# Tile 0's tokens in strips of 32 partitions: packed state products and updates, conv on unfolded copies

## The reference, cut to what matters

```python
cross = jnp.einsum('bhqd,bhdv->bhqv', q * q_dec[None, :, :, None], s)
s_new = (jnp.exp(c * log_g)[None, :, None, None] * s
         + jnp.einsum('bhkd,bhkv->bhdv', k * k_dec[None, :, :, None], v))
...
u = u_a * jax.nn.sigmoid(u_b)
ext = jnp.concatenate([conv_buf.astype(u.dtype), u], axis=1)
c = lax.conv_general_dilated(ext, conv_w[:, None, :], ...)
```

## Time and profile before

| | |
|---|---|
| runs, median | 1305.79 us (1303.9 to 1307.8) |
| profiled execution | 1306.49 us |
| its span in the trace | 1304.7 us |
| mean granted TensorE clock | 0.962 |
| PE busy | 1186.6 us, 91% |
| VectorE busy | 996.3 us, 76% |
| ACT busy | 632.8 us, 48% |
| POOL busy | 121.9 us, 9% |

### The profile page before, as it was taken

The page is one execution under the profiler, slowest core; times in us unless marked ns, Lnnn a source line. Parts: engine busy times, 40 slices in busy tenths (PEclk is TensorE's granted clock), DMA queues, the critical chain, the costliest instruction groups (busy, mean ns, idle before and its releaser), DMA issues.

```text
span 1304.7 us, 15355 instructions
## 1 busy us (share of the span) xinstructions
PE 1186.6 (91%) x5825; PEld 909.9 (70%) x5825; DVE 996.3 (76%) x1301; ACT 632.8 (48%) x565; POOL 121.9 (9%) x216
## 2 busy tenths in 40 slices
PE   3999999999999999999736999999999999999960
PEld 3985986798589759998524767676767677676740
DVE  3598779778986986465644888888888888888846
ACT  2350324134122502453114777777777777777740
POOL 3111020112012011000030000000000000000012
PEclk9999999999999999999857999999999999999985
DMA  8565483466347545345345999999999999999934
GB/s 213 179 209 193 125 262 125 178 201 234 117 178 228 196 176 174 129 129 192 130 134 211 356 373 380 388 377 381 381 382 379 381 380 380 381 382 380 388 95 109
DMA packets 171052, 332.25 MB, mean 255 GB/s; under 512 B 8154, under 2 KB 45322, under 8 KB 170960
## 3 DMA queue, kind: packets, MB, share of 16 engines
q1 hardware_dynamic: 150576, 264.41, 57.9%
q0 software_dynamic: 20400, 66.81, 15.2%
HBM read 295.28 MB, written 36.63 MB: 254 GB/s over the span
## 4 chain that ended last, share of the span: by engine, by line
PE 84%; DVE 7%; DMA 3%; ACT 3%; issue 2%; POOL 2%; POOLq 0%; DVEq 0%; ACTq 0%
PE bank L676 77%; PE bank L888 4%; PE bank L717 3%; DMA v2rows<-in_b_conv_o_dram 1%; DVE o_tok L1360 1%; DMA x_slots<-x,slot 1%; DMA y_back<-y_slots,slot 1%; DVE sg_lo L1374 1%; DVE sg_f L1372 1%; POOL x_slots L633 1%; ACT sg_hi L1074 1%; DMA y_slots<-yo 0%; POOL vrows L520 0%; DVE stats L1351 0%; DVE lo L996 0%
## 5 line engine op out<-in xcount | busy, mean ns | idle before, releaser
L1516 DVE TENSOR_TENSOR mlo<-mraw,mhi 128x2048 fp32r<-128x2048 f32 x192 | 439.5, 2290 | 79.1 <-ACT mhi L1140 75.8
L1140 ACT ACTIVATE mhi<-mraw 128x2048 fp32r<-128x2048 f32 x192 | 367.5, 1915 | 93.8 <-PE bank L676 83.7
L676 PE MATMUL bank<-mhi,xg_hi 128*96 128x512 f32 x512 | 203.2, 397 | 1.4 <-DVE xg_lo L1521 1.4
L676 PE MATMUL bank<-mhi,xg_lo 128*96 128x512 f32 x512 | 203.0, 397 | 0.0
L676 PE MATMUL bank<-mlo,xg_hi 128*96 128x512 f32 x512 | 201.7, 394 | 0.0
L996 DVE TENSOR_TENSOR lo<-raw,hi 128x2048 fp32r<-128x2048 f32 x56 | 128.3, 2290 | 83.2 <-ACT hi L1103 38.7
L991 ACT ACTIVATE hi<-raw 128x2048 fp32r<-128x2048 f32 x47 | 90.0, 1914 | 191.4 <-PE bank L676 191.4
L676 PE MATMUL bank<-xT_hi,hi 128*128 128x336 f32 x512 | 165.3, 323 | 6.4 <-DVE lo L996 6.4
L676 PE MATMUL bank<-xT_hi,lo 128*128 128x336 f32 x512 | 163.1, 319 | 0.0
L676 PE MATMUL bank<-xT_lo,hi 128*128 128x336 f32 x512 | 163.0, 318 | 0.0
L1269 DVE SCALAR_TENSOR_TENSOR cT<-E,hv,cT 128x272 f32<-128x272 f32 x480 | 150.3, 388 | 0.0
(11 more groups left out here) (245 smaller groups left out, 1572.9 us busy)
## 6 DMA issues: line engine op xcount, KB each, us to landing
mraw<-in_w_gate_dram SPq DMA_DIRECT2D x64, 1024.0 KB, 11.2
mraw<-in_w_up_dram SPq DMA_DIRECT2D x64, 1024.0 KB, 11.1
mraw<-in_w_down_dram SPq DMA_DIRECT2D x64, 1024.0 KB, 11.9
raw<-in_w_in_dram SPq DMA_DIRECT2D x40, 1024.0 KB, 5.3
st<-in_state_ret_dram POOLq DMA_DIRECT2D x32, 512.0 KB, 4.8
out_dram<-st POOLq DMA_DIRECT2D x32, 512.0 KB, 3.9
raw<-in_w_ret_o_dram SPq DMA_DIRECT2D x8, 1024.0 KB, 7.1
x_slots<-zeros POOLq DMA_DIRECT2D x12, 512.0 KB, 4.7
```

The costliest lines, as they stand in the source:

```text
L676: i = pe.matmul(out, a, b, start=s, stop=e)
L1140: act.activation(mhi[:, v % MH, :], mraw[:, v % MR, :], ACT.Copy).then_inc(mhi_ready, 1)
L1516: dve.tensor_tensor(mlo[:, v % MH, :], mraw[:, v % MR, :], mhi[:, v % MH, :].bitcast(f32), ALU.subtract).then_inc(mlo_ready, 1)
```

## The change

The tokens of tile 0 are put in another order: strip c (partitions 32c to 32c + 31) holds samples c and c + 4 in its first 16 places and, for c under 3, 16 prompt tokens behind them. Tile 0 still has 112 tokens. Tables follow (`token_order`); loads and stores of x and y for tile 0 become one per sample, one for the meta tokens, one for each 16 prompt tokens.

The state product takes 16 columns of `qdiag` a sample, into partitions 32c of the bank, four strips after one another for each r (sample c + 4r) and p. The state update asks for room for the four groups of an (r, p) first, then issues for each of the three terms four matmuls, each contracted over one strip's 32 rows; `kds` has one column of the table for each r, so 2 in place of 8.

The conv reads `W`, in which each 8 tokens have a window of their own with the 30 values before them (42 windows of 38): a tap is one instruction of 336 elements. VectorE writes u into the windows' ends with one instruction a half; ACT makes from it `us`, the prompt's stream `E`, and from that the first 30 places of the prompt's windows.

```diff
-        kds_hi = sb("kds_hi", [TT, NB, 256], f32r)
+        kds_hi = sb("kds_hi", [TT, 2, 256], f32r)
-        qdiag = sb("qdiag", [128, 2, NB * (NS + NI)])
+        qdiag = sb("qdiag", [128, 2, NB, QC])
...
-                     + [f"Pst{b}{p}" for b in range(NB) for p in range(2)]
+                     + [f"Pst{c + 4 * r}{p}" for r in range(2) for p in range(2) for c in range(4)]
...
+        def windows(c):
+            return W[:, c, :].rearrange("p (n w) -> p n w", n=NW)
+
+        def prompt_windows(c, j0, j1):
+
+            a = E[:, c, NI * j0:NI * j1 + CW - 1 - NI]
+            return bass.AP(a.tensor, a.offset, [list(a.ap[0]), [NI, j1 - j0], [1, CW - 1]])
+
+        def seq_windows(c):
+
+            w = windows(c)
+            return w[:, 0:16, :].rearrange("p (c r) w -> p c r w", c=4)[:, :, 0:2, :]
...
-            sp.dma_start(x_in[0:NS, 0, :], x_sample.rearrange("b i d -> (b i) d")).then_inc(s_x, 16)
-            sp.dma_start(x_in[NS:NS + NM, 0, :], meta_tokens).then_inc(s_x, 16)
-            sp.dma_start(x_in[NS + NM:TT, 0, :], x_prompt[0, 0:TT - NS - NM, :]).then_inc(s_x, 16)
+            for b in range(NB):
+                sp.dma_start(x_in[place(b):place(b) + NI, 0, :], x_sample[b]).then_inc(s_x, 16)
+            sp.dma_start(x_in[16:32, 0, :], meta_tokens).then_inc(s_x, 16)
+            for c in range(1, 3):
+                sp.dma_start(x_in[32 * c + 16:32 * c + 32, 0, :], x_prompt[0, 16 * c - NM:16 * c + 16 - NM, :]).then_inc(s_x, 16)
...
-                for c in range(2):
-                    pe.wait_ge(evac[HEAD.bank[f"ua{c}"]], HEAD.used(f"ua{c}", h) + 1)
+                pe.wait_ge(stream_ready, h * 2 + 2)
...
-                        o64 = bank[HEAD.bank[name]][0:NS, :]
-                        for b in range(NB):
+                        for r in range(2):
                             for p in range(2):
-                                i = pe.matmul(o64, qdiag[:, p, b * NS:(b + 1) * NS], st[:, b, p, :], start=False, stop=(b == NB - 1 and p == 1), skip_group_check=True)
+                                for c in range(4):
+                                    i = pe.matmul(bank[HEAD.bank[name]][32 * c:32 * c + QC, :], qdiag[:, p, c + 4 * r, :], st[:, c + 4 * r, p, :],
+                                                  start=False, stop=(r == 1 and p == 1), skip_group_check=True)
                         i.then_inc(group_done, 1)
...
-                for b in range(NB):
+                for r in range(2):
                     for p in range(2):
-                        name = f"st{b}{p}"
-                        room(HEAD, name, h)
-                        out, cols = bank[HEAD.bank[name]][:, :], slice(p * 128, (p + 1) * 128)
-                        group(HEAD, name, h, [(out, kds_hi[:, b, cols], v_hi[:, :], True, False), (out, kds_hi[:, b, cols], v_lo[:, :], False, False),
-                                              (out, kds_lo[:, b, cols], v_hi[:, :], False, True)])
+                        cols = slice(p * 128, (p + 1) * 128)
+                        for c in range(4):
+                            room(HEAD, f"st{c + 4 * r}{p}", h)
+                        for n, (a, v) in enumerate(((kds_hi, v_hi), (kds_hi, v_lo), (kds_lo, v_hi))):
+                            for c in range(4):
+                                rows = slice(32 * c, min(32 * c + 32, TT))
+                                i = pe.matmul(bank[HEAD.bank[f"st{c + 4 * r}{p}"]][:, :], a[rows, r, cols], v[rows, :], start=n == 0, stop=n == 2)
+                                if n == 2:
+                                    i.then_inc(group_done, 1)
...
+                for c in range(2):
+                    act.wait_ge(*took(HEAD, f"ua{c}", h))
+                    act.activation(us[:, c, :].rearrange("p (r c i) -> p c r i", r=2, c=4), seq_windows(c)[:, :, :, CW - 1:WW], ACT.Copy)
+                    act.activation(E[:, c, CW - 1:CW - 1 + 48].rearrange("p (c r i) -> p c r i", c=3, r=2), early_windows(c)[:, :, :, CW - 1:WW], ACT.Copy)
+                    act.activation(E[:, c, CW - 1 + 48:EXT].rearrange("p (n i) -> p n i", i=NI), windows(c)[:, 14:NW, CW - 1:WW], ACT.Copy).then_inc(stream_ready, 1)
+                    act.wait_ge(stream_ready, h * 2 + (c + 1))
+                    act.activation(early_windows(c)[:, :, :, 0:CW - 1], prompt_windows(c, 0, 6).rearrange("p (c r) w -> p c r w", c=3), ACT.Copy)
+                    act.activation(windows(c)[:, 14:NW, 0:CW - 1], prompt_windows(c, 6, 34), ACT.Copy).then_inc(windows_ready, 1)
...
-                for s in range(NB):
+                for s in range(2):
                     i = act.activation(kds_hi[:, s, :], b[0:TT, 0:256], ACT.Copy, scale=hs[0:TT, HKS + s:HKS + s + 1])
...
-                parts = [(out[:, NS:T], lambda w: E[:, c, EL + w:EL + w + NP]),
-                         (out[:, 0:NS].rearrange("p (b i) -> p b i", b=NB), lambda w: samples(E[:, c, :])[:, :, w:w + NI])]
                 for w in range(w0, w1):
                     tap = hv[:, VCW + c * CW + w:VCW + c * CW + w + 1]
-                    for q, (o, src) in enumerate(parts):
-                        if w == 0:
-                            ins = dve.tensor_scalar(o, src(w), tap, hv[:, VCB + c:VCB + c + 1], ALU.mult, ALU.add)
-                        else:
-                            dve.wait_ge(dve_step, conv_last[q])
-                            ins = dve.scalar_tensor_tensor(o, src(w), tap, o, ALU.mult, ALU.add)
-                        conv_last[q] = count(ins)
+                    src = windows(c)[:, :, w:w + NI]
+                    if w == 0:
+                        ins = dve.tensor_scalar(out, src, tap, hv[:, VCB + c:VCB + c + 1], ALU.mult, ALU.add)
+                    else:
+                        dve.wait_ge(dve_step, conv_last[0])
+                        ins = dve.scalar_tensor_tensor(out, src, tap, out, ALU.mult, ALU.add)
+                    conv_last[0] = count(ins)
...
-                for s in range(NB):
+                for r in range(2):
                     for p in range(2):
-                        b, e = full(HEAD, f"st{s}{p}", h)
-                        dve.scalar_tensor_tensor(st[:, s, p, :], st[:, s, p, :], hs[:, HGAM:HGAM + 1], b[:, :], ALU.mult, ALU.add).then_inc(e, 1)
+                        for s in range(4 * r, 4 * r + 4):
+                            b, e = full(HEAD, f"st{s}{p}", h)
+                            dve.scalar_tensor_tensor(st[:, s, p, :], st[:, s, p, :], hs[:, HGAM:HGAM + 1], b[:, :], ALU.mult, ALU.add).then_inc(e, 1)
```

89 lines of the change are left out of this document (55 added, 34 removed).

## The result

The kernel after takes 1326.79 us (median of 4 runs, 1325.79 to 1327.39), the kernel before, run beside it, 1306.32 (1303.9 to 1307.8): a ratio of 1.0158, 95% interval 1.014 to 1.0175. The change costs 20.5 us. The profiled execution took 1327.39, its span is 1325.5 (1304.7 before), and the mean granted clock fell from 0.962 to 0.921.

What follows compares the result with a forecast made beforehand. TensorE is nearly always busy, but VectorE reaches o0 together with it and is the chain in the state updates. -3.9 + 8.2 + 1.5 = +5.8 a head, with the start 24.2 in all: 1331 us, range 1308 to 1356.

Steps and rivals of the forecast that it cites:

- VectorE before o0: From v_tok to o0's statistics: 34 conv taps save 0.7 us, fewer kds_lo 2.4, less 0.1: 3.0 us a head.
- wait for o1: VectorE's 0.93 us wait for o1 disappears in each head because TensorE finishes its products sooner.
- four rounds: State updates: PE and VectorE alternate over four banks, 4.7 us a round at half clock, 18.7 for 10.5: +8.2 a head.
- behind the updates: Prompt-state products after the state updates begin at the low clock and lengthen by 1.2 to 2.2 us: +1.5 a head.
- start, once: Kernel start: eight more SP loads at 0.59 us delay x_in and the first weights: +1.0 us once, between 0 and 4.7.
- State product: 32 matmuls in four column strips before o0: half packed, 7 us for 13.95; anything below about 11 worth the same.
- The rival's 0.48: Conv: dependent taps run as close as independent ones, 0.48 us apart; 1300, or 1295 with perfect packing; chance 0.09.
- the total of 1326: State-update rounds by the Trainium skill's packing rule: 4.4 us a round at half clock, total near 1326 us.
- Clock: State-update rounds: half clock expected in all four after PE's long wait; +8.2 us a head, against +5.7 at full clock.
- Edits off the path: ACT copies, POOL loads and stores, y stores: hidden behind idle stretches or waits; nothing, at most 2 us for stores of y.
- strips don't pack: State product and updates: fp32 strips run one after another; +9.9 a head, 1347, or 1386 with the clock fallen; chance 0.12.
- The clock holds: State-update rounds stay at full clock: +1.8 us a head, 1315, or 1309 to 1310 with perfect packing; chance 0.18.

Runs made afterwards that it cites:

- the run by strip: The kernel after with the sixteen state products ordered strip by strip instead of the four strips in turn: 1326.4 us.
- the kernel with three edits: The kernel after with rounds on two sets of banks, taps of the halves in turn, and the eight sample loads on ScalarE's queue: 1282.8 us.
- the kernel with four names: The kernel after with stand-in matmuls to hold the clock, 36 ahead of the rounds and 8 in each, spread over four F-bank names: 1311.0 us.
- the last kernel: The kernel with three edits plus overwritten stand-in matmuls in the rounds' own banks, 20 before the first round, 6 before each later: 1281.2 us.
- one name: The kernel after with stand-in matmuls to hold the clock, 36 ahead of the rounds and 8 in each, under one added F-bank name: 1322.3 us.

## Why the prediction was right, point by point

The forecast was 1331, the time is 1326.8. The mechanism was the one named: the state updates in four bunches and the half clock stand in the trace, and the taps are 0.60 us apart for the 0.59 forecast. Little of the nearness is luck: three terms were off by more than 0.1 us, the rounds and the stretch behind them (too long, together 1.2 us a head) and the start (too short, 1.1 once). The terms of a head:

| term | forecast | measured, head 1 |
|---|---|---|
| VectorE before o0 | -3.0 | -3.1 |
| wait for o1 | -0.9 | -0.9 |
| four rounds | +8.2 | +7.55 |
| behind the updates | +1.5 | +0.95 |
| a head | +5.8 | +4.5 |
| start, once | +1.0 | +2.1 |

*State product: a wrong step, without effect.* "An fp32 product is two instructions for the same strip, so the second cannot start before the first ends" led to half packing, 7 us. It took 3.63: with the strips in turn, four matmuls go in the time of one (8 x 0.43 = 3.5). The premise that only neighbours in issue order can run side by side is wrong as well: in the run by strip, by its loads, each strip runs half beside the next, with all eight of its matmuls ahead of the next's in the program. The prediction had said that anything below 11 us is worth the same, and the run by strip bears it out at 8.80 us.

*VectorE before o0.* The distance fell by 3.06 for the 3.0 of the sum, 0.7 of it in the taps and 2.35 in kds_lo, as forecast. The tap was the important choice: the durations alone promised 6 us, the 0.03 of the earlier trace rows gave 0.59, and 0.60 was measured. The rival's 0.48 was also real, but for taps that do not wait for their neighbour; the kernel after does not have them. Of the Trainium skill, VectorE: DVE Perf Modes, section "The DRAIN you can't avoid", says of chained VectorE instructions that leaving out the semaphores between them gains nothing, measured there on eight copies, and also that "A next op that is not held starts earlier". Here they come closer by 0.12 us an instruction when the wait is for the one before last instead of the last. That agrees with the second sentence and not with the first: the measurement decides.

*Rounds.* 4.52 us and not 4.7. The spacing was the mis-sized term: the step from one term's four strips to the next's is 0.57 and 0.43 us at the half clock (238.25, 238.82, 239.25) where 4 x 0.15 = 0.60 was put. At the full clock, 3.83 was measured and 4.06 forecast. The rule of the Trainium skill (TensorE: Matmul & The Clock Gate, "Measured speedup vs the span model"), a pack in little more than the time of one matmul, agrees with these two steps, 0.46 us being one matmul at the half clock. That the total of 1326 worked out by it met the time is in part luck: its rounds (+7.1) come near the +7.55 measured, but the 0.55 us a head by which the tail was too long and the 1.1 by which the start was too short are in it as well and cancel in part.

*Clock.* It fell as expected and cost 3.95 us a head (15.8 in all), where the forecast had 8.2 - 5.7 + 1.5 = 4.0. The parts were 2.5 in the rounds and 1.5 behind them, against 2.75 and 1.0 measured.

*Tail.* The prompt-state products were 1.1 us longer, of the 1.2 to 2.2 put down; the clock came back in their middle.

*Start.* The mis-sized term with the other sign. SyncE's queue took 2.72 us for the eight loads, 0.34 each, where 0.59 was taken from the earlier trace rows, and the last load of x_in left it 2.3 us later (6.77 and 4.44); but x_in was complete 6 us later (18.04, and 12.09 in the earlier trace rows), not 4.7 at most, and the vectors' transposes behind its own, at 20.41 before, began at 22.54. The issue alone does not explain it: with the eight loads on ScalarE's queue, SyncE's last load of x_in left it at 4.12, sooner than in the kernel before, and x_in was still complete only at 15.13 (13.87 in the kernel with three edits). That the small loads make the others land later is the likely reading; it was not measured by itself.

*Edits off the path.* ScalarE's copies and the extra stores cost nothing that the trace shows. v_tok waits 1.85 us for TensorE, 1.74 in the kernel before, so the copies did not come too late.

Of the rivals, "strips don't pack" is out by the trace. "The clock holds", forecast at 1315, is the kernel with four names: 1311.0, below by the packing that it had priced too high (3.83 and not 4.06 a round, sixteen rounds).

## What to carry to other kernels

When work is issued in batches, count the buffers that a batch takes: here a batch as large as the ring made producer and consumer take turns, at the half clock and at the full one. A faster producer ahead of a consumer that arrives at the same moment gained nothing itself, but it made the gain of the consumer count (14.7 us with it, nothing without), so try the two together before you judge either. And an experiment that adds one name to a rotation, or one instruction to an engine's written order, changes more than it says: look at what stands behind it.

## What was not expected of the hardware

- Column strips with fp32 products pack fully when they are issued in turn (3.63 us for 32 matmuls, 0.11 each), and only in part when each strip's eight follow one another (8.80, 0.275 each: each strip beside the last four matmuls of the one before). The first was thought impossible; why the overlap is four is not explained.
- Row strips run side by side at the half clock too: the third term's four start 0.43 us after the second's, where a single matmul is 0.23 at the full clock, so 0.46 at the half. They do so too when a strip's three terms stand together in the program, and then TensorE starts the next strip's first (232.01) ahead of this one's third (232.37).
- Whether a VectorE instruction waits for its neighbour's result or for the one before that is worth 0.12 us each (0.60 against 0.48) at an equal duration: 14.7 us of this kernel, by order alone.
- TensorE kept the full clock with gaps of 0.3 to 0.9 us between bursts (the last kernel) and with one of 1.50 (four names). It lost it in one long gap (the kernel after, idle from 228.5; 0.85 in the window 231 to 232, 0.50 in the next), but also behind one of 1.84 us (one name; 1.00 up to 277, 0.50 from 277.5 on, with the matmuls running again since 276.94).
